# Block inverses of two chunked recurrences: blocks gathered side by side, transposed on all partitions, and other due times for the split panels

## The reference, cut to what matters

```
a_mat = where(strict, einsum('bhncd,bhnjd->bhncj', k_beta, kc) * decay, 0.0)
sol = triangular_solve(eye + a_mat, rhs, left_side=True, lower=True, unit_diagonal=True)
```

```
sa = einsum('bhij,bhj->bhi', state, -kk_t)
state = state * d_t[:, :, None, :] + sa[..., None] * (kk_t * a_t)[:, :, None, :] + v_t[..., None] * k_t[:, :, None, :]
y_t = einsum('bhij,bhj->bhi', state, r_t)
```

## Time and profile before

| | us |
|---|---|
| median of 3 runs | 2142.48 (2141.2 to 2143.66) |
| the profiled execution | 2142.85 |
| its span | 2141.0 |
| PE busy | 2031.1 (95%) |
| DVE / ACT / POOL busy | 909.1 / 804.8 / 982.3 |
| TensorE clock granted, mean | 0.977 |

### The profile page before, as it was taken

How to read it: one execution, slowest core, us unless ns; L and a number is a source line. 1 busy time by engine, 2 the same in 40 slices (tenths; PEclk the granted TensorE clock), 3 DMA queues, 4 the chain that set the end, 5 groups by cost and what they waited for, 6 DMA issues and landing times.

```text
span 2141.0 us, 26269 instructions
## 1 busy us (share of the span) xinstructions
PE 2031.1 (95%) x10166; PEld 1639.2 (77%) x10166; DVE 909.1 (42%) x1508; ACT 804.8 (38%) x1057; POOL 982.3 (46%) x766
## 2 busy tenths in 40 slices
PE   6997899999999999999999888989999999999997
PEld 3785896875778887888888576966887788888886
DVE  1679554766433044232200587457944452111101
ACT  3565224346554224222222543343225743222221
POOL 3636613644313464655555373013443265565652
PEclk9998999999999999999999899999999999999999
DMA  6311104721112332222233211011222222222222
GB/s 274 99 60 59 40 1 200 277 79 40 47 53 79 113 123 79 95 92 92 97 117 115 92 60 60 2 50 40 99 79 79 81 98 99 99 99 99 98 99 79
DMA packets 29482, 194.87 MB, mean 91 GB/s; under 512 B 5040, under 2 KB 7216, under 8 KB 8752
## 3 DMA queue, kind: packets, MB, share of 16 engines
q1 hardware_dynamic: 29360, 193.19, 24.8%
HBM read 188.99 MB, written 4.19 MB: 90 GB/s over the span
## 4 chain that ended last, share of the span: by engine, by line
PE 81%; DVE 12%; ACT 3%; DMA 2%; POOL 1%; issue 1%; SPq 0%; ACTq 0%; DVEq 0%; POOLq 0%
PE ps L411 22%; PE ps L412 21%; PE ps L413 21%; PE ps L471 2%; DVE ar L2391 1%; DVE sm L2390 1%; DMA ar<-ada_dram 1%; DVE ar L1844 1%; POOL WL L2476 1%; PE ps L827 1%; PE ps L840 1%; PE ps L501 1%; DVE ar L1870 1%; PE ps L895 1%; DVE ar L1944 1%
## 5 line engine op out<-in xcount | busy, mean ns | idle before, releaser
L2476 POOL TENSOR_TENSOR WL<-raw,WH 128x512 fp32r<-128x512 f32 x588 | 774.1, 1317 | 951.5 <-ACT WH L1278 915.3
L411 PE MATMUL ps<-hH,WH 128*128 128x512 f32 x1648 | 662.1, 402 | 27.9 <-POOL WL L2476 6.6
L413 PE MATMUL ps<-hH,WL 128*128 128x512 f32 x1648 | 648.4, 393 | 0.0
L412 PE MATMUL ps<-arR,WH 128*128 128x512 f32 x1392 | 542.5, 390 | 0.0
L1278 ACT CAST WH<-raw 128x2048 fp32r<-128x2048 f32 x147 | 280.8, 1911 | 503.5 <-DMA raw<-panels_dram 501.9
L411 PEld LDWEIGHTS ps<-hH,WH 128*128 128x128 f32 x1648 | 313.9, 190 | 110.3 <-issue 36.1
L413 PEld LDWEIGHTS ps<-hH,WL 128*128 128x128 f32 x1648 | 313.7, 190 | 67.3
L412 PE MATMUL ps<-xL,WH 128*128 128x512 f32 x848 | 336.6, 397 | 0.0
L412 PEld LDWEIGHTS ps<-arR,WH 128*128 128x128 f32 x1392 | 262.0, 188 | 54.3 <-issue 0.2
L411 PE MATMUL ps<-arR,WH 128*128 128x512 f32 x592 | 230.6, 390 | 1.4 <-DVE ar L1927 1.4
L413 PE MATMUL ps<-arR,WL 128*128 128x512 f32 x592 | 230.3, 389 | 0.0
(11 more groups left out here) (376 smaller groups left out, 2230.2 us busy)
## 6 DMA issues: line engine op xcount, KB each, us to landing
raw<-panels_dram SPq DMA_DIRECT2D x145, 1024.0 KB, 4.8
ar<-ada_dram SPq DMA_DIRECT2D x12, 2048.0 KB, 12.0
xT<-xT_dram SPq DMA_DIRECT2D x2, 2048.0 KB, 9.4
out_dram<-xT SPq DMA_DIRECT2D x8, 512.0 KB, 2.6
xT<-out_dram SPq DMA_DIRECT2D x1, 2048.0 KB, 10.8
wide<-wide_dram SPq DMA_DIRECT2D x1, 1024.0 KB, 6.7
raw<-panels_dram SPq DMA_DIRECT2D x1, 992.0 KB, 5.7
raw<-panels_dram SPq DMA_DIRECT2D x1, 960.0 KB, 6.0
```

What stands on the lines that cost most here:

```text
L411: mm(out, lhs[0], rhs[0], start=first, stop=False)
L412: mm(out, lhs[0], rhs[1], start=False, stop=False)
L413: return mm(out, lhs[1], rhs[0], start=False, stop=final)
L2476: ins = tt(WL[:, n % SLOTS, c], raw[:, n % SLOTS, c], WH[:, n % SLOTS, c].bitcast(F32), ALU.subtract)
```

## The change

It has four parts. (1) `unit_inverses` no longer gathers the blocks itself. After each tile t ACT copies the diagonal blocks side by side into "squares" (`gather`, four copies of 32x256), DVE transposes them on all 128 partitions in two calls, and transposes back out of PSUM in two calls. In the first recurrence the result stays as squares and XTR is a product of a constant with a broadcast of them; in the second ACT copies it back to the diagonal (`scatter`), tile by tile, and PE's `invert_0` waits for each tile. One more tile, EXTRA, is allocated. (2) The sums `l2` 8 to 15 and the projections `qkv` 16 to 18 use other banks. (3) A panel's due step is the smaller of the former one and six steps after the release of the slot's last panel (`LANDED`). (4) The order of some work is moved: `rkv` 3 before the products `rm`, `nv` 3 behind the first `invert_0`, the number of substitution steps between convolutions and mixes, the place of the gatherings, and the look-aheads of POOL.

```
-            return 0 if n < 2 else panel_part[0] if n == 2 else panel_part[n - SLOTS + 1]
+            return 0 if n < 2 else panel_part[0] if n == 2 else min(panel_part[n - SLOTS + 1], panel_release[n - SLOTS] + LANDED)
...
+LANDED = 6
-STEP_BANKS, OUT_BANKS = (0, 1, 2, 3), (4, 5)
+STEP_BANKS, OUT_BANKS, SUM_BANKS = (0, 1, 2, 3), (4, 5), (1, 2, 4, 5)
-        RW_AX, RW_T, RW_TD, KRT, RW_LOW, RW_PRODUCT = 36, 24, 25, 22, 22, 24
+        RW_AX, RW_T, RW_TD, KRT, RW_LOW, RW_PRODUCT = 36, EXTRA, 25, 22, 22, 24
+        SQUARES, RW_SQUARES = (19, 48), (24, 24)
+        def by_block(x):
+            return x.rearrange("p h (g c) -> p h g c", c=32)
+        def repeated(t, hf):
+            return squares32(EXTRA - 1 if t >= 2 else SQUARES[1], t, HALF, HALF * hf).unsqueeze(2).to_broadcast([P, HALF, 4, 32])
+        def same_block():
+            return const("same32").rearrange("p (g c) -> p g c", c=32).unsqueeze(1).to_broadcast([P, HALF, 4, 32])
+        def squares32(i, t, n=8, n0=0):
+            c0 = 256 * (t % 2) + 32 * n0
+            return tile(i + t // 2)[:, c0:c0 + 32 * n].rearrange("p (n c) -> p n c", c=32)
+        def squares_by_column(i, half):
+            return ar[:, i:i + 2, :].rearrange("p a (n c) -> p c (a n)", c=32)[:, 16 * half:16 * half + 16, :]
+        def diagonal32(base, q, t):
+            x = ar[:, base + 2 * t:base + 2 * t + 2, :].rearrange("p a (h c) -> p (a h) c", c=P)
+            return x[32 * q:32 * q + 32, :, 32 * q:32 * q + 32]
...  PE, block_1
-                        column_sums("l2", n, [tile(24 + n % 4)], [(sem("l2_sq"), n + 1)], banks=ALL_BANKS if g < 2 else CHAIN_BANKS)
+                        column_sums("l2", n, [tile(24 + n % 4)], [(sem("l2_sq"), n + 1)], banks=ALL_BANKS if g < 2 else SUM_BANKS)
-                project("qkv", h_mix, 1, i0=16, banks=CHAIN_BANKS)
+                project("qkv", h_mix, 1, i0=16, banks=(0,))
                 unit_sums(2)
-                project("qkv", h_mix, 1, i0=17, banks=CHAIN_BANKS)
+                project("qkv", h_mix, 1, i0=17, banks=(3,))
                 unit_sums(3)
-                project("qkv", h_mix, 1, i0=18, banks=CHAIN_BANKS)
+                project("qkv", h_mix, 1, i0=18, banks=(0,))
...  PE, block_2
-                project("rkv", h_mix, 2, i0=1)
+                project("rkv", h_mix, 3, i0=1)
-                project("rkv", h_mix, 1, i0=3, banks=CHAIN_BANKS)
-                later_values(3)
                 def invert_0(t):
                     pe.wait_ge(sem("rw_cleared"), t + 1)
+                    pe.wait_ge(sem("rw_solved"), t + 1)
-                pe.wait_ge(sem("rw_solved"), 1)
                 invert_0(0)
+                later_values(3)
                 invert_0(1)
...  ACT
+            def gather(base, squares, t, done):
+                for q in range(4):
+                    ins = nc.scalar.copy(squares32(squares, t)[32 * q:32 * q + 32], diagonal32(base, q, t))
+                    if q < 3:
+                        link(ins)
+                link(ins, sem(done), t + 1)
+            def scatter(base, squares, t, blocks_job, done):
+                for b in range(2):
+                    emptied(act, blocks_job, b)
+                for q in range(4):
+                    ins = nc.scalar.copy(diagonal32(base, q, t), squares32(squares, t)[32 * q:32 * q + 32])
+                    ...
                     conv_tap(11 + t)
+                    if t:
+                        act.wait_ge(sem("ax_made"), t)
+                        gather(AX, SQUARES[0], t - 1, "ax_gathered")
+                act.wait_ge(sem("ax_made"), NT)
+                gather(AX, SQUARES[0], NT - 1, "ax_gathered")
...  ACT, block_2: after kaprow 1 scatter 0; after kaprow 3 scatter 1; after invert_1 corners and scatter of 2 and 3
+                scatter(RW_AX, RW_SQUARES[1], 0, "rw_blocks", "rw_solved")
...  DVE
+                dve.wait_ge(sem(gathered), NT)
+                for b in range(2):
+                    link(v.transpose(low3[:, 16 * b:16 * b + 16, :], squares_by_column(squares[0], b)))
...
                 for b in range(2):
-                    link(v.tensor_copy(lower[:, b, :], unit[:, b, :]), *read(blocks_job, b))
-                for q in range(4):
-                    ins = v.transpose(blocks(ar[:, base:base + 8, :], q), low3[32 * q:32 * q + 32, :, :])
+                    link(v.transpose(squares_by_column(squares[1], b), unit3[:, 16 * b:16 * b + 16, :]), *read(blocks_job, b))
...  steps of the first inverses, with conv 15 to 18 between: 7, 6, 6, 6, 7 become 1, 8, 7, 7, 9
-                    link(tt(pair(XTR, hf), pair(AX, hf), bm(const("same32")), ALU.mult), sem("gdn_xtr"), 1 + hf)
+                    link(tt(by_block(pair(XTR, hf)), repeated(0, hf), same_block(), ALU.mult), sem("gdn_xtr"), 1 + hf)
+                link(v.tensor_copy(tile(EXTRA), tile(SQUARES[1] + 1)), sem("squares_kept"), 1)
...  block_2: mix 6 and 7 behind the products with the norms, mix 8 behind the first mask, tell("rw_made") after each
...  POOL
-                        filled(pool, "l2", n - 4)
+                        pool.wait_ge(pe_done, last["l2", n - 4])
-                    if n in SPLIT_AFTER:
+                    if n in SPLIT_AFTER[:-2]:
                         ahead(pool, "qkv", QKV_ORDER[n + 1])
+                ahead(pool, "l2", 11)
-                pool.wait_ge(sem("ax_ready"), 1)
+                pool.wait_ge(sem("ax_made"), NT)
...
-            for i in (46, 47, 12, 13):
+            for i in (RW_T, 46, 47, 12, 13):
                 ins = g.memset(tile(i), 0.0)
```

More of the change, by code:

```diff
@@ L275, in tile @@
         def tile(i):
+            if i == EXTRA:
+                return extra[:]
             if i >= 50:
@@ L303, in build @@
         Q0, K0, V0 = 0, 8, 16
+        EXTRA = 54
         AX, ATT, XTR, XX, MK, P1 = 32, 40, 24, 26, 28, 30
@@ L1640, in block_2 @@
                 ahead(act, ("rm", 0, 0))
+                for t in range(NT):
+                    act.wait_ge(sem("rw_made"), t + 1)
+                    gather(RW_AX, RW_SQUARES[0], t, "rw_gathered")
                 for p in range(4):
@@ L1678, in block_2 @@
                 copied(in_place(KAP, 3), ("kaprow", 3))
-                copied(tile(NVT[3]), ("nv", 3))
+                scatter(RW_AX, RW_SQUARES[1], 1, "rw_blocks", "rw_solved")
                 def invert_0(t):
@@ L1699, in block_2 @@
                 invert_0(0)
+                copied(tile(NVT[3]), ("nv", 3))
                 invert_0(1)
@@ L1706, in block_2 @@
                     corners(2 + t)
+                    scatter(RW_AX, RW_SQUARES[1], 2 + t, "rw_blocks", "rw_solved")
                 for t in range(NT):
@@ L1867, in unit_inverses, with steps @@
                 for b in range(2):
-                    link(v.tensor_copy(lower[:, b, :], unit[:, b, :]), *read(blocks_job, b))
-                for q in range(4):
-                    ins = v.transpose(blocks(ar[:, base:base + 8, :], q), low3[32 * q:32 * q + 32, :, :])
-                    if q < 3:
-                        link(ins)
-                link(ins, sem(done), 1)
+                    link(v.transpose(squares_by_column(squares[1], b), unit3[:, 16 * b:16 * b + 16, :]), *read(blocks_job, b))
                 yield
+            def steps(units, n):
+                for _ in range(n):
+                    next(units)
             def attention(name, units, scale, smt, bias, between):
@@ L2261, in masked @@
                         link(tt(pair(dst, par), heads4((what, t, par)), bm(const(mask)), ALU.mult), *read((what, t, par)))
-                dve.wait_ge(sem("kt_ready"), 4)
+                mix(6)
+                mix(7)
                 for t in range(NT):
+                    if t == 2:
+                        dve.wait_ge(sem("kt_ready"), 4)
                     masked(RW_AX + 2 * t, "rm", t, "strict64")
-                units = unit_inverses(RW_AX, RW_LOW, RW_PRODUCT, "rw_blocks", "rw_solved")
-                next(units)
-                mix(8)
+                    tell(sem("rw_made"), t + 1)
+                    if t == 0:
+                        mix(8)
+                units = unit_inverses(RW_LOW, RW_PRODUCT, RW_SQUARES, "rw_blocks", "rw_gathered")
+                steps(units, 1)
                 mix(9)
-                for _ in range(5):
-                    next(units)
+                steps(units, 2)
                 mix(10)
-                for _ in range(3):
-                    next(units)
+                steps(units, 6)
                 mix(11)
-                for _ in range(3):
-                    next(units)
+                steps(units, 5)
                 mix(12)
-                for _ in range(3):
-                    next(units)
+                steps(units, 4)
                 mix(13)
-                for _ in range(3):
-                    next(units)
+                steps(units, 2)
                 for p in range(4):
@@ L2286, in block_2 @@
                     link(tt(tile(BV + p), pst("bon", p), tile(V2 + p), ALU.mult), *read("bon", p))
```

(7 more changed lines are left out.)

50 lines of the change are left out of this document (18 added, 32 removed).

## The result

The changed kernel takes 2150.07 us, the median of 5 runs (2147.06 to 2155.14); the kernel before took 2142.48 beside it (2141.20 to 2143.92). The ratio is 1.0032, with a 95% interval from 1.0016 to 1.0048: slower by 7.6 us by the medians, where 9 us of gain were forecast. The profiled execution took 2148.51 with a span of 2146.7, against 2142.85 and 2141.0 before; so the profiles hold 5.7 of the 7.6 us.

The account below looks back on a forecast made before the run. PE, busy 95% of the span, was taken as the bound, so only its idle stretches and clock losses could be won. From 2142.85: -9.2 - 4 - 9.6 + 4.8 + 4.3 + 4.5 gives 2133 us; range 2128 to 2139, with rivals 2121 to 2142.

Parts of the forecast that it names:

- The first block inverses: First recurrence: cheaper DVE transposes, no wait at l2 10, project 19 at 191.0 instead of 198.99; gain 9.2 us.
- 12 if that bank is free early: First block inverses: upper case, gain 12 us if bank 4, which project 19 needs, is free early.
- The three stalls: Early panels 28 (key norms), 33 and 109 (ends of the two attentions): costs 4.8, 4.3 and 4.5 us.
- Panel 90's gap: Before ai 1: panel 90 due earlier removes PE's 6.61 us gap and its slow clock; gain 9.6 us.
- The second block inverses: Second recurrence: gain 4 us from 1333.18, with nv 0 at 1313 to 1315 behind 6 us of PE idleness.
- 8 if the memsets aren't late: Second block inverses: upper case, gain 8 us if POOL's memsets before nv 0 are not late.
- the bound of 1.5: Second block inverses: lower case, gain only 1.5 us if clock and scatters add up.
- DVE's saving of 7 us: Second block inverses, behind nv 0: DVE saves the last copies and transposes, 1.4 + 8.1 - 2.1 = 7 us.
- rival 2: Splits before copies decide: early splits cost their upper ends, nv 0 late, second stage loses 3; 2145 us, chance 0.07.
- rival 3: DVE transposes cost by the call: first stage gains 6, second 0; 2140 us, chance 0.10.
- rival 1: PE's clock holds over the 3.6 to 5 us gaps: costs shrink by 6, RWKV gain grows by 2; 2125 us, chance 0.22.
- rival 4: The splits do not stall, as loads land sooner or look-ahead falls elsewhere: costs 0 to 4; 2121 us, chance 0.10.

Follow-up runs that it names:

- e9: e6 with the projections qkv 19 and 20 in banks 3 and 5 in place of bank 4 for project 19: 2118.98 us, ratio 0.9884.
- e3: The changed kernel with the old due times for panels 28, 33 and 109 alone, panel 90 still early: 2132.58 us, ratio 0.9948.
- e1: The changed kernel with the old due formula for all panels: 2140.23 us (12 runs), ratio 0.9973.
- e8: The kernel before with one edit, panel 90 due with u 1 0 in the middle of the RWKV chain: 2133.34 us, ratio 0.9952.
- e2: The kernel before with the new due formula alone, old inverses kept: 2162.5 us, ratio 1.0084.
- e5: e3 with POOL's five memsets put between the splits of panels 89 and 90, not behind both: 2124.81 us, ratio 0.9918.
- e6: e4 with ACT's scatter of tile 1 behind the x0 copies of tile 0, and nv 3 in bank 0: 2119.09 us, ratio 0.9891.
- e4: e3 with panel 90 due with u 1 0, in the RWKV chain, instead of with gup 1: 2124.37 us, ratio 0.9912.
- e7: The changed kernel with LANDED = 12 in place of 6: 2132.33 us, ratio 0.9950.

## Why the prediction was wrong

**The first block inverses: right.** -9.4 us against -9.2. No idleness at l2 10; project 19 at 190.05 (191.0 forecast) behind 4.67 us, released by ACT's logarithm; the low clock behind it (0.50 up to 195.8). The transposes were sized right: rows of 128x512 at 1.12 and 1.15 us, 2.2 ns for each element of a partition where the old ones took 2.0 (1.03 us taken), and XTR was ready at 201.2 (201.7). These are DVE's groups from 161 to 212 us:

```profile
L2083 DVE TENSOR_TENSOR ar<-ar,cm 128x512 f32<-128x512 f32 x2 | 2.4, 1179 | 0.1
L1925 DVE STREAM_TRANSPOSE ar<-ps 128x512 f32<-128x512 f32 x2 | 2.3, 1145 | 0.1
L1912 DVE STREAM_TRANSPOSE ar<-ar 128x512 f32<-128x512 f32 x2 | 2.2, 1116 | 1.2 <-ACT ar L1416 1.1
```

What I said of an early bank ("12 if that bank is free early") was wrong: in e9 it is 0.7 us at x0 of tile 1, and nothing that the medians can tell.

**The three stalls: right in place and mechanism, a little small.** Forecast 4.8, 4.3 and 4.5; by the shifts 6.0, 5.1 and 4.5; by e3 17.5 together in the medians. Behind all three the granted clock was 0.50, up to 516.7, 646.4 and 1707.9. At the key norms the split stands where I had it, between the third and the fourth square, and PE resumed within 1 us of the forecast: 513.09, which with the shift of 11.5 is 524.6 on the old time, against 524.0. My list of the panels that move left out two, 26 and 87; PE has no idleness of 0.3 us between 464 and the key norms, where 26 is split, and from 1187 to the gup products, where 87 is, e1 takes the same time within 0.5 us, so they cost nothing that shows.

**Panel 90's gap: right.** 9.6 forecast, 9.7 by e8's median and 9.4 by its timeline.

**The second block inverses: the step that failed.** I wrote "From 1333.18 I get 4 us of gain", with nv 0 at 1313 to 1315 and PE idle for 6 us before it. From 1187 to the gup products the gain is there (-3.0): `rkv` 3 stands before the products `rm`, and these start behind 1.57 us and at a clock of 1.00, where before it was 5.29 and 0.50. The gap of 3 us that I saw there came as two, these 1.57 and 1.91, with the low clock behind the second (0.50 up to 1271.0). nv 0 came at 1315.91 behind 7.84, near what I had. What I got wrong is what a late nv 0 does to all that stands behind it. The sum took "8 if the memsets aren't late" down to 4, so it priced them at 4 us. The runs show four things in its place:

- Behind 7.84 us the clock is low, 0.50 up to 1322.2 (the row 0.54). I had that only in the bound of 1.5, not in the sum.
- DVE's last steps and transposes are queued behind a mask that waits for a product behind nv 0. So DVE's saving of 7 us ended in the 11.52 us wait: its transposes end 27.9 us behind the gup products, where they ended 28.3 behind them before, and x0 starts 30.0 behind them. In e1, with nv 0 in time, x0 starts 21.6 behind them.
- On ACT two scatters of 1.70 stand in front of the x0 copies, and the bank of nv 3 hangs on these: 3.03 us and again a low clock (0.50 up to 1342.7). I had the two scatters, again only in that bound, but not that nv 3's bank hangs on them.
- 2.6 us came from a clock that fell behind a gap of 1.03 (below).

Together +7.9 from 1187 to the sums instead of -4. The profiles give each part its size, from one execution of each kernel (e1's is the lowest of its twelve). The stretch takes 226.8 us before, 234.7 in the changed kernel and 225.4 in e1, which has the memsets in time. So the late memsets cost 9.2 us where I had priced 4 (in e2, with the old inverses, the stretch is 11.7 longer than before, 2.6 of it that clock). And without them the stage gains 1.3 where I had 8; 2.6 of what is missing is the clock of the last point, and the gap of 3 us before nv 3 with its low clock is in e1 as well (3.00, and 0.50 up to 1323.8). 5.2 and 6.7 are the 11.9 by which the stage was missed. For the place of panel 90 on POOL the medians say nearly 8 (e5 against e3); for ACT's order they say 5 (e6 against e4), of which the profiles show less.

**The rest of the miss.** The profile lies 14.9 us above the forecast: 11.9 here, 2.0 in the three stalls, 1.9 in the stretch with panel 90's gap (the slow sums), and -0.9 in all other places together, of which +1.7 between the first index product and the last turned scores and -1.0 before 56 us have no cause that a run shows.

**What that makes of the rivals.** The mechanism of rival 2 (early splits decide, made heavier by the late `mk_zero`) is the one that came about, to which I gave 0.07 and 2145. Its upper ends for the three stalls were 18.1 together; the table has 15.6 and e3 17.5 to 18.1. Its mistake was mine: "with a slow clock: the second stage loses 3", where it lost 7.9. Transposes by the call (rival 3) and a clock that holds (rival 1) are excluded by the rows above; rival 4 by the three gaps.

**Still open.** The medians differ by 7.6 us and the profiles by 5.7; e1 has two groups of runs, 7 us apart. Gaps in the profiles that come and go in the same code are of that size (one of 5.3 us near 431 us in e3 and e5, of 3.4 in e6, none there in e4), but no pair of profiles of e1 shows it.

## What to carry to other kernels

A split, a cast or any piece of look-ahead work that is let into an in-order queue earlier cost in these runs about its full length or more wherever the next instruction of that queue was one that the bottleneck waited for (a cast of 1.9 us cost 2 in e7, and 5.1 and 4.5 at the ends of the attentions; a split of 5.3 us nearly 8), and the clock fell to 0.50 behind the gaps of 3.03, 3.45, 3.71 and 7.84 us. So choose such a due time by the idle stretch in the timeline of each engine that does a part of it (POOL was idle for 96 us behind the place where panel 90's split cost 8), and not by a constant number of steps from the release. And when a wait grows, do not book a saving of another engine on top before you have looked at what is queued behind that wait: a saving that ends inside a wait is nothing.

## What the runs showed of the hardware

The same three groups of PE with the same 1.03 us gap before them, at the end of the recurrence, took 1.09 us each in some executions and 1.97 in others: in the changed kernel, in e1, e2 and e4 the clock fell there to 0.50, in e5 and e7 0.4 us further on, and in the kernel before, e3, e6, e8 and e9 it held at 1.00. This is the first group in the kernel before; the changed kernel's is the row at 1414.36 above:

```profile
1409.84 1.09 PE L1017 MATMUL ps<-ar 128*64 128x128 f32 x8 [1.03 <-DVE ar L2329]
```

It costs 2.6 us up to the sums of the group norm and 1.8 in them. One execution is not enough to give or take 4.4 us at such a place.

How long the low level lasts differs as much. Behind 7.84 us the changed kernel was back at 1.00 at 1322, after some 6 us of work. Behind 7.83 us e3 worked at 0.50 from 1305.70 to 1335, though PE was busy all the time up to a gap of 1.47 us at 1327.4. In e3's busy time by stretch the clock is again the third number from the end:

```profile
1310.00:1325.00 15.00, 15.00 (x83) 13.89 (x83) 6.76 (x14) 5.22 (x12) 0.00 (x0) 0.50 0.01 2
```

So the 3 us that the prediction took for each fall of the clock is what the falls of the kernel before cost (behind 4.19, 5.29 and 6.61 us, 0.50 for 5.0, 5.2 and 6.0 us of work), and not a bound.

DVE's copy of 128x512 out of SBUF (L2084) took 1.38 to 1.40 us in all eight profiles that have it, twice the 0.69 of the copies out of PSUM; POOL's mask products ran beside it each time (200.74 to 203.79 in the changed kernel). It stands behind XTR and hid there. No run here has the copy without POOL beside it, so what makes it that long is not shown.
